# Retention over records kept on chip, with scores one step ahead and one summed result per tile, and an expert-choice search done in halves

## What is computed

```python
def step(state, qkv):                      # retention, one chunk
    qc, kc, vc = qkv
    s = jnp.einsum('bhid,bhjd->bhij', qc, kc) * intra
    o = jnp.einsum('bhij,bhjv->bhiv', s, vc) + jnp.einsum('bhid,bhdv->bhiv', qc, state) * xi
    state = state * decay_chunk + jnp.einsum('bhjd,bhjv->bhdv', kc * zeta, vc)
    return state, o

ret = head_group_norm(o_f, gn_g) * jax.nn.silu(gf) \
    + head_group_norm(o_b, gn_g) * jax.nn.silu(gb)      # forwards plus backwards
out = jnp.concatenate([ret, conv], axis=-1) @ w_out

cap = max(1, (EC_CAPACITY_FACTOR * n) // N_EXPERTS)     # 128 latent, 32 context tokens
aff = jax.nn.softmax(jnp.einsum('bnd,de->bne', h, router_w), axis=-1)
gates, idx = lax.top_k(aff.transpose(0, 2, 1), cap)     # 16 experts
```

## Time and profile before

| | us |
|---|---|
| median of three runs | 3380.14 (3379.59 to 3390.08) |
| the profiled execution, its own time | 3382.69 |
| span of the profiled execution | 3380.9 |
| retention stage within the span | about 513 to 673 |
| `mixer_out`, `routing` of the first layer | about 673 to 856, 856 to 924 |
| `mixer_out`, `routing` of the second layer | about 2568 to 2705, 2705 to 2769 |
| busy: PE, DVE, ACT, POOL | 2924.2, 2080.8, 1409.5, 520.6 |

### The profile page before, as it was taken

One profiled execution on the slowest core, in us unless ns is written; L12 is line 12 of the kernel. 1 busy time (PEld: TensorE's weight loads), 2 busy tenths in 40 slices (PEclk: granted clock), 3 DMA queues, 4 the chain that ended last, 5 costly groups with the idle time before them and its releaser, 6 DMA issues. The chain is left out here.

```text
span 3380.9 us, 51489 instructions
## 1 busy us (share of the span) xinstructions
PE 2924.2 (86%) x19792; PEld 2312.1 (68%) x19792; DVE 2080.8 (62%) x2164; ACT 1409.5 (42%) x1717; POOL 520.6 (15%) x487
## 2 busy tenths in 40 slices
PE   6999995688099999999949997799997819999998
PEld 3766785667078888888835554688886708777776
DVE  3577825654766666666712232566664488888887
ACT  2212114432055555555512334344332217777675
POOL 0000004511012122212214446000000001111111
PEclk8999997899599999999979999899998959999999
DMA  5368616653467788778641223522203349999995
GB/s 214 125 211 267 218 60 250 221 184 128 171 224 279 284 308 283 280 284 304 222 167 45 69 66 95 157 81 61 70 21 112 119 183 359 377 375 373 370 378 174
DMA packets 160338, 690.25 MB, mean 204 GB/s; under 512 B 14337, under 2 KB 78849, under 8 KB 124514
## 3 DMA queue, kind: packets, MB, share of 16 engines
q1 hardware_dynamic: 145634, 650.97, 52.8%
q0 software_dynamic: 14592, 37.76, 4.7%
HBM read 600.50 MB, written 88.18 MB: 204 GB/s over the span
## 5 line engine op out<-in xcount | busy, mean ns | idle before, releaser
L1784 DVE TENSOR_TENSOR ex_wlo<-ring,ex_whi 128x2048 fp32r<-128x2048 f32 x384 | 877.2, 2289 | 264.9 <-ACT ex_whi L1711 260.8
L1711 ACT CAST ex_whi<-ring 128x2048 fp32r<-128x2048 f32 x384 | 727.5, 1905 | 251.1 <-PE psum L1676 250.8
L1676 PE MATMUL psum<-ex_whi,ex_xh 128*128 128x512 f32 x1024 | 411.4, 402 | 10.8 <-DVE ex_wlo L1784 10.8
L1676 PE MATMUL psum<-ex_wlo,ex_xh 128*128 128x512 f32 x1024 | 401.2, 392 | 0.0
L1676 PE MATMUL psum<-ex_whi,ex_xl 128*128 128x512 f32 x1024 | 400.8, 391 | 0.0
L1676 PEld LDWEIGHTS psum<-ex_whi,ex_xh 128*128 128x128 f32 x1024 | 193.5, 189 | 61.6 <-DVE ex_wlo L1784 14.8
L529 PE MATMUL psum<-fr_whi,fr_hh 128*128 128x512 f32 x560 | 223.8, 401 | 12.9 <-DVE fr_hl L713 11.5
L1676 PEld LDWEIGHTS psum<-ex_whi,ex_xl 128*128 128x128 f32 x1024 | 193.4, 189 | 41.8
L1676 PEld LDWEIGHTS psum<-ex_wlo,ex_xh 128*128 128x128 f32 x1024 | 193.7, 189 | 37.2
L529 PE MATMUL psum<-fr_wlo,fr_hh 128*128 128x512 f32 x560 | 218.1, 391 | 0.7 <-DVE fr_wlo L719 0.7
L529 PE MATMUL psum<-fr_whi,fr_hl 128*128 128x512 f32 x560 | 218.1, 391 | 0.0
(11 more groups left out here) (278 smaller groups left out, 5235.8 us busy)
## 6 DMA issues: line engine op xcount, KB each, us to landing
ring<-in_moe_w SPq DMA_DIRECT2D x192, 2048.0 KB, 9.8
fr_raw<-in_mod_w SPq DMA_DIRECT2D x40, 1024.0 KB, 5.7
ring<-rec_d SPq DMA_DIRECT2D x20, 1024.0 KB, 7.1
rec_d<-fr_work SPq DMA_DIRECT2D x72, 256.0 KB, 5.8
fr_raw<-in_ev_w_in SPq DMA_DIRECT2D x14, 1024.0 KB, 5.6
h_d<-ring SPq DMA_DIRECT2D x18, 512.0 KB, 3.0
fr_arena<-in_mod_w SPq DMA_DIRECT2D x8, 1024.0 KB, 13.8
ring<-mod_d SPq DMA_DIRECT2D x11, 512.0 KB
```

What stands on the lines that cost most here:

```text
L1676: last = nc.tensor.matmul(g.psum[:, 2 + i % 2, :], x[:, 4 * b + k, :], w[n][:, k, :], start=(b == 0 and k == 0 and first == 0), stop=(b == ...
L1711: nc.scalar.copy(whi[m % RING][:, :, :], slot(i)[:, 4 * b:4 * b + 4, :]).then_inc(hi_set, 1)
L1784: nc.vector.tensor_tensor(wlo[n][:, :, :], slot(i)[:, 4 * b:4 * b + 4, :], whi[n][:, :, :].bitcast(F32), ALU.subtract).then_inc(lo_set, 1)
```

## The change

Retention. The ten records lie on chip in ten places of their own, each loaded once and used by both directions; the code is written out for ten steps instead of a loop. The first two tiles' records are loaded ahead of everything but two small tables. The output projection's weights, which were loaded first, now come in two halves of 2 MB behind step 2 and step 7, into places that records have left. Scores, masks and scaled queries of step i+1 are made in step i, into two buffers; decayed keys are made a step ahead; the state has two buffers. The normalisation and the gating of a step are written into the next step on ACT and POOL. In steps 0 and 2 to 5 a direction is the first to reach its tile and its gated result goes straight into a total; in step 1 and steps 6 to 9 it is the second, and POOL adds the two (L1088 after). The total, one tensor for each tile, is stored once.

`mixer_out`. It loads that one result for each tile and has no sum of its own; PE's and ACT's lists of steps are written out instead of looped.

`routing`. The latent tokens lie in two halves of 512 on 16 partitions each (0 to 15 and 32 to 47), the context tokens on partitions 64 to 79. A round is one instruction of each kind over all of them, 512 columns wide. Each half gives its 128 best; the second list is reversed, and place by place the larger of the two is taken, which gives the 128 best of both. The order of the tokens within an expert's list is then another one.

Of retention only the lines that the changed kernel has are shown, since those that they replace stand in the function above.

```diff
+        TREC = 4 * HALF
+        order = [[XT, XT + 1] + list(range(XT)), [XT + 1, XT] + list(reversed(range(XT)))]
+        slots = [8, 9, 3, 4, 0, 7, 1, 6, 2, 5]
+        rec = {t: g.ring[:, n * TREC:(n + 1) * TREC] for n, t in enumerate(slots)}
+        total = [uf[:, t * HALF:(t + 1) * HALF] for t in range(NT)]
...
+            return i == 1 or i >= 2 + XT // 2
...
+                load_rec(XT)
+                load_rec(XT + 1)
                 sp.dma_start(ln[:, :], io["conv_ln"]).then_inc(ln_in, 16)
+                for i in range(2):
+                    for d in dirs:
+                        load_gate(d, i)
+                for i in range(2, 2 + XT // 2):
+                    for d in dirs:
+                        load_rec(order[d][i])
                 sp.dma_start(g.router[:, :], io["router_w"][0]).then_inc(g.wout_in, 16)
+                for i in range(NT):
+                    sp.wait_ge(c_done, i + 1)
+                    sp.dma_start(rows(io["mix_d"], i)[:, HALF:D], mixc[i % 2][:, :]).then_inc(mixc_out[i % 2], 16)
+                    if i == 2:
+                        for d in dirs:
+                            sp.wait_ge(out_sum[d], 2)
+                        load_wout(0)
+                    if i == 7:
+                        for d in dirs:
+                            sp.wait_ge(out_sum[d], 7)
+                        load_wout(1)
                     for d in dirs:
+                        if i >= 1 and i + 1 < NT:
+                            load_gate(d, i + 1)
+                    if i and second(i - 1):
+                        for d in dirs:
+                            t = order[d][i - 1]
+                            sp.wait_ge(added[d], seconds(i - 1))
+                            sp.dma_start(rows(io["mix_d"], t)[:, 0:HALF], total[t]).then_inc(total_out, 16)
...
+                    scores(0, d)
+                for i in range(NT):
+                    if i + 1 < NT:
+                        for d in dirs:
+                            scores(i + 1, d)
+                    pe.wait_ge(c_cut, i + 1)
+                    if i:
+                        pe.wait_ge(c_normed, i)
+                    transpose_tile(nc, g, 6, ys, range(4)).then_inc(c_turned, 1)
+                    if i + 1 < NT:
+                        for d in dirs:
+                            keys_values(i, d)
                     for d in dirs:
+                        outputs(i, d)
+                    pe.wait_ge(c_normed, i + 1)
+                    if i:
+                        pe.wait_ge(c_done, i)
                     transpose_tile(nc, g, 7, yn, range(4)).then_inc(c_back, 1)
...
+                    mask(0, d)
+                for i in range(NT):
                     for d in dirs:
+                        if i + 1 < NT:
+                            mask(i + 1, d)
+                        if d == 0 and i:
+                            shifted(i - 1, 1)
+                    dve.wait_ge(c_turned, i + 1)
                     nc.vector.bn_stats(cst[:, :], g.psum[:, 6, :]).then_inc(c_stat, 1)
+                    dve.wait_ge(c_stat, 2 * i + 1)
+                    if i:
+                        dve.wait_ge(c_root, 2 * i - 1)
                     nc.vector.bn_aggr(cmv[:, :], cst[:, :]).then_inc(c_stat, 1)
+                    if i + 1 < NT:
+                        update(i, 0)
+                    dve.wait_ge(c_root, 2 * i + 2)
+                    if i:
+                        dve.wait_ge(c_normed, i)
                     nc.vector.scalar_tensor_tensor(cnm[:, :], cmv[:, 0:1], -1.0, crs[:, :],
                                                    ALU.mult, ALU.mult).then_inc(c_shift, 1)
+                    if i + 1 < NT:
+                        update(i, 1)
                     for d in dirs:
+                        moments(i, d)
+                    shifted(i, 0)
...
+                    if not second(i):
+                        nc.gpsimd.tensor_tensor(total[t], xh[d][:, :], gate[d][b], ALU.mult).then_inc(gated[d], 1)
+                        return
+                    nc.gpsimd.tensor_tensor(xh[d][:, :], xh[d][:, :], gate[d][b], ALU.mult).then_inc(gated[d], 1)
+                    pool.wait_ge(gated[d], i + 1)
+                    met = order[1 - d].index(t)
+                    pool.wait_ge(gated[1 - d], met + 1)
+                    nc.gpsimd.tensor_tensor(total[t], total[t], xh[d][:, :], ALU.add).then_inc(added[d], 1)
...
+                    decayed_keys(0, d)
+                for i in range(NT):
+                    if i:
+                        gated_output(i - 1, 0)
+                    pool.wait_ge(c_stat, 2 * i + 2)
+                    if i:
+                        pool.wait_ge(c_root, 2 * i)
+                    nc.gpsimd.tensor_scalar(cve[:, :], cmv[:, 1:2], EPS, None, ALU.add).then_inc(c_root, 1)
+                    pool.wait_ge(c_root, 2 * i + 1)
+                    if i:
+                        pool.wait_ge(c_normed, i)
+                    nc.gpsimd.tensor_tensor(crs[:, :], cve[:, :], g.mhalf[:, 0:1], ALU.pow).then_inc(c_root, 1)
+                    if i + 2 < NT:
+                        for d in dirs:
+                            decayed_keys(i + 1, d)
+                    if i:
+                        gated_output(i - 1, 1)
                     for d in dirs:
+                        roots(i, d)
+                for d in dirs:
+                    gated_output(NT - 1, d)
...
+                cut(0)
+                for i in range(NT):
+                    if i:
+                        normalise(i - 1, 1)
+                    act.wait_ge(c_shift, i + 1)
...
+                    normalise(i, 0)
+                normalise(NT - 1, 1)
...
-                        sp.dma_start(rf[b], rows(io["ret_d"][0], rt)).then_inc(r_in[b], 16)
-                        sp.dma_start(rb[b], rows(io["ret_d"][1], a.t + CT)).then_inc(r_in[b], 16)
+                        sp.dma_start(ret[b], rows(io["mix_d"], a.t)[:, 0:HALF]).then_inc(r_in[b], 16)
...
-                def add(a):
-                    pool.wait_ge(r_in[a.b], 32 * (a.i + 1))
-                    pool.wait_ge(r_turned, a.t + 1)
-                    nc.gpsimd.tensor_tensor(rsum, rf[a.b], rb[a.b], ALU.add).then_inc(r_sum, 1)
...
+                for r in range(rounds):
+                    n = nr if r < rounds_c else 48
+                    a, v, i = g.affT[0:n, :], val[0:n, 8 * r:8 * r + 8], idx[0:n, 8 * r:8 * r + 8]
+                    if r:
+                        dve.wait_ge(found, 3 * r)
+                    nc.vector.max(v, a).then_inc(found, 1)
+                    dve.wait_ge(found, 3 * r + 1)
+                    nc.vector.max_index(i, v, a).then_inc(found, 1)
+                    dve.wait_ge(found, 3 * r + 2)
+                    nc.vector.match_replace(a, v, a, -1.0).then_inc(found, 1)
+                dve.wait_ge(found, 3 * rounds)
+                for m, table in enumerate((idx, val)):
+                    nc.vector.tensor_copy(rank[0:32, m, :], table[0:32, :]).then_inc(rank_set, 1)
+                    nc.vector.tensor_copy(rank[32:48, m, :], table[32:48, ::-1]).then_inc(rank_set, 1)
+                if ctx:
                     for m, table in enumerate((idx, val)):
                         nc.vector.tensor_copy(four[:, m, :].rearrange("e (q t) -> e q t", q=4),
-                                              table[:, CAPX:].unsqueeze(1).to_broadcast([NE, 4, CAPC])).then_inc(idf_set, 1)
+                                              table[64:64 + NE, 0:CAPC].unsqueeze(1).to_broadcast([NE, 4, CAPC])).then_inc(
+                                                  rank_set, 1)
                 dve.wait_ge(turned, 1)
-                nc.vector.tensor_copy(g.gate_x[:, :], g.psum[:, 0, NE:2 * NE]).then_inc(tabled, 1)
-                nc.vector.tensor_copy(g.idx_x[:, :], g.psum[:, 0, 0:NE]).then_inc(tabled, 1)
-                if layer == 0:
+                nc.vector.tensor_copy(both[:, :, 0:48], g.psum[:, 0, 0:128].rearrange("p (m n) -> p m n", m=2)[:, :, 0:48]
+                                      ).then_inc(chosen, 1)
+                dve.wait_ge(chosen, 1)
+                ia, ib, va, vb = both[:, 0, 0:NE], both[:, 0, 32:48], both[:, 1, 0:NE], both[:, 1, 32:48]
+                nc.vector.tensor_tensor(better[:, :], va, vb, ALU.is_ge).then_inc(chosen, 1)
+                nc.vector.scalar_tensor_tensor(step[:, :], ia, float(-half), ib, ALU.add, ALU.subtract).then_inc(chosen, 1)
+                nc.vector.tensor_tensor(g.gate_x[:, :], va, vb, ALU.max).then_inc(tabled, 1)
+                dve.wait_ge(chosen, 3)
+                nc.vector.tensor_tensor(step[:, :], step[:, :], better[:, :], ALU.mult).then_inc(chosen, 1)
+                dve.wait_ge(chosen, 4)
+                nc.vector.scalar_tensor_tensor(step[:, :], step[:, :], float(half), ib, ALU.add, ALU.add).then_inc(chosen, 1)
+                dve.wait_ge(chosen, 5)
+                nc.vector.tensor_copy(g.idx_x[:, :], step[:, :]).then_inc(tabled, 1)
```

440 lines of the change are left out of this document (189 added, 251 removed).

## The result

| | before | after |
|---|---|---|
| median | 3379.86 us (3377.04 to 3390.08, 4 runs) | 3304.85 us (3300.34 to 3311.27, 4 runs) |
| profiled execution, span | 3382.69, 3380.9 | 3300.34, 3298.3 |
| retention | 159.8 | 131.0 |
| first `mixer_out` | 183.4 | 173.9 |
| first search, to the last index | 66.6 | 40.15 |

The ratio is 0.9772 (95% interval 0.975 to 0.9795): faster, 8.9 us above the 3296 that was forecast and within the range. The stage times are differences of instants in the two profiled executions; each row runs between the same two instructions before and after (retention from its first load to the first load of `mixer_out`, a search from its first pass to the instruction that writes the last indices).

The account below looks back on a forecast made before the run. Retention was taken as bound by a loop of keys, gate product, load, landing and scores, the search by DVE. Retention -23, `mixer_out` -9.6 and search -51.9 sum to -84.5 on 3382.7; against the median 3296 us, range 3284 to 3311.

Parts of the forecast that it names:

- Retention's steps: Steps 1 to 9 of retention: 97.0 us for 118.4, plain steps 10.1 and steps with sums 11.7, a gain of 21.4.
- the two waits: POOL's waits in a plain retention step: 0.3 us for ACT's gate input and 1.5 for DVE's convolution aggregate.
- the 4.5 us for the low clock: Added to retention's steps, 0.5 us a step, for PE products running at the lower clock.
- Start: Retention up to its first root: with records loaded first the root comes at 542.1 for 544.4, -2.3 us.
- End: Retention behind its last root: two sums come in, partly beside ACT, +0.9 us.
- `mixer_out`: First `mixer_out`: no POOL sum beside the norm product, 8.1 us from eight tiles and 1.5 at the start, -9.6.
- The 1.5 us for the start: Start of the first `mixer_out`: four L1291 take 6.91 us beside the first sum, against 5.2; 1.5 taken as gain.
- Search: Both searches: passes over 512 columns, rounds of 2.26 us for 3.87, +1.3 each behind them; together -51.9 us.
- the old bound: Retention before: a loop of keys, gate product, load, landing and scores sets the step, 13.15 us a turn.
- Rival B: Retention moves to another limit, PE's low clock or masks waiting for scores; it gives 5 us, time 3314; chance 0.10.
- C: Search passes don't shrink with columns: cost by partition group, 3313, or passes kept at 1.2 us, 3348; chance 0.06.
- D: Retention's gate loads come late on SP's queue, POOL waits every step; at 22 us a step 3399; chance 0.015.

## Why the prediction was right, step by step

In the profiled executions the change gives 82.4 us where 84.5 were summed. The rest of the distance to 3296 is that before's profiled execution lay 2.5 us above the median that the prediction used and after's 4.5 below its own; by the medians the change gave 75.0 us. That 82.4 is so near to 84.5 is partly luck: retention gave 5.8 us more than the 23 forecast, and what lies outside the sum took about as much back.

- **Retention's steps**: 94.3 for 97.0. The plain step of 10.1, 11.7 in the sum steps and the two waits came as written, though not every part: the gate product L1082 or L1084 took 1.27, not 1.5, and the gaps of about 0.08 between POOL's instructions, which the walk left out, made up for it. Steps 8 and 9, 10.7 and 9.4, were 1.1 and 0.4 longer: with no keys due POOL waits 1.00 us in step 8 for DVE's moments, and the walk had looked at POOL alone there. What was mis-sized is the 4.5 us for the low clock, for which no sign is left: plain steps are at 10.14 without it. The mean clock is 0.93 in the steps (537 to 632 us) and 0.86 in the stage; in the kernel before they were 0.86 and 0.79. The Trainium skill, "TensorE: Matmul & The Clock Gate", section "HAM oscillation — how this bites in real kernels", describes bursts that start low behind waits for transfers; the trace agrees in that both fell together, the waits for records from 50.5 to 12.9 us and the share of low clock.
- **Start**: -4.5 for -2.3, counted from the stage's first load (31.05 to 26.53). The first mask stands 6.1 us earlier where 5.5 were forecast, and from it to the first root are 1.5 us more where 3.2 were charged for the next step's products; by the run with scores in their own step these cost 2.1. **End**: 10.2 for 10.35, no change where +0.9 was forecast.
- **`mixer_out`**: -9.6, as forecast, but partly by luck. The 1.01 us in each of eight tiles came, and the run with the sum put back bears that mechanism out. The 1.5 us for the start did not: the first norm product starts 31.3 us behind the stage's first load, for 30.6. In their place the first two tile intervals gave 2.6 and 1.4, not 1.0 each, from something that the sum did not name.
- **Search**: 26.4 + 23.7 = 50.1 for 51.9. A round took 2.30 for 2.26, and what stands behind the rounds grew by 1.9 us in the first search, not 1.3. The line was drawn through passes on 16 partitions; at 256 columns a pass takes 0.42 on 48 partitions where it took 0.40 on 16.
- **Mechanism, the old bound**: the prediction named a loop through keys, gate product and load. With the scores ahead, late loads cost a whole landing in each step; that is shown. That freeing the load alone would have done is refuted by the run with the gate products first. That it needed the keys' new place as well is argued. The 13.15 us of a turn were also a mean: five of the nine steps before took 11.2 to 12.7 us and four 14.0 to 15.8, and POOL's keys waited for a record only five times in them, 8.7 us in all.
- **Rival B** (clock or masks as the next limit) did not come, nor **C**; **D** neither, POOL waited for no gate. Of C's first form, a cost by partitions, some 0.02 us a pass is there.
- **What was outside the sum**: +2.1 us ahead of the first gather, +6.2 between the latents and the second search, -1.9 in the front. The second may be chance, but the kernel before and its variant have 981.4 and 980.4 us there and the ten kernels with the change 981.6 to 987.6, so some of it may come with the change; that is open. The gap ahead of the gather is 3.9 to 4.2 us in the kernel after and four variants (6.6 with 256 columns) and 1.9 in before and five others, those in which POOL's list has another length; why is open, and the prediction had said that the gathers start at once.

## What to carry to other kernels

When a wait for a load closes a loop, look what else is in that loop before cutting it: the same load freed by order alone made the kernel slower, since another chain was longer. Behind such a change walk the next engine's list instruction by instruction with its waits; that gave the plain and the sum steps to 0.1 us, and missed step 8 by 1.1 where only one engine was walked. A wait left in the walk (1.46 us) was the next gain. Working ahead costs code and a start; try the steady steps without it.

## What the runs showed of the hardware

- MAX8, FIND_INDEX8 and MATCH_REPLACE8 take 0.69, 0.68 and 0.67 us for 512 columns on 48 or 80 partitions, and 1.2 for 1024 on 16. At 256 columns MAX8 takes 0.396 on 16, 0.420 on 48 and 0.424 on 80. So time goes by columns, and more partitions cost 0.03 at most.
- A POOL sum with both sources the same tile took 1.04 us for 1.29 with two, and a DVE product that began 0.07 us behind it lost 0.77 for 1.01. The Trainium skill, "SBUF — State Buffer", section "SBUF: two separate sides", has one wait for the other's whole instruction; here the loss was about 0.2 us less than what was left of the sum both times.
